# A two-layer decoder step: keys ahead of the last input units, queries scaled in PSUM reads, gates split inside attention, V pages by GpSimd, the norm unit by unit

## What is computed

```
for layer in (0, 1):
    h = rms_norm(x, g_mix)
    q, k, v, ... = split(h @ w_in)            # layer 0: forget gate, u, v_g; layer 1: gate_b, gate_c, h_in
    a = attention(q, cached pages + k, v)     # 0: softmax with forget sums; 1: stick-breaking
    b = u * spatial(layer_norm(v_g))          # 1: gate_b * short_conv(gate_c * h_in)
    x = x + concat(a, b) @ w_out
    x = x + square(relu(rms_norm(x, g_mlp) @ w_up)) @ w_down
y = rms_norm(x, g_final); k, v, forget gates and states are outputs as well
```

## Time and profile before

| | us |
|---|---|
| three runs, median (lowest, highest) | 1667.32 (1666.06, 1671.25) |
| the profiled execution, its span | 1666.99, 1665.3 |
| PE busy, of the span | 1542.4 (93%) |
| DVE, ACT, POOL busy | 729.8, 493.6, 57.9 |
| PE idle before matmuls, largest groups | 15.1 + 13.6 + 13.2 + 8.1 + 7.9 + 7.7 + 7.6 + 7.3 + 7.2 |
| mean granted clock | 0.965 |
| HBM read, written | 170.20 MB, 7.26 MB |

### The profile page before, as it was taken

One profiled execution on the slowest core, in us unless ns is written; L12 is line 12 of the kernel. 1 busy time (PEld: TensorE's weight loads), 2 busy tenths in 40 slices (PEclk: granted clock), 3 DMA queues, 4 the chain that ended last, 5 costly groups with the idle time before them and its releaser, 6 DMA issues.

```text
span 1665.3 us, 33771 instructions
## 1 busy us (share of the span) xinstructions
PE 1542.4 (93%) x13119; PEld 1445.1 (87%) x13119; DVE 729.8 (44%) x1267; ACT 493.6 (30%) x787; POOL 57.9 (3%) x130
## 2 busy tenths in 40 slices
PE   5879979978999999999999995987899999999997
PEld 5879946658999999999999994655799999999996
DVE  4335456534444333343443364656244433434333
ACT  4211234422333222231321113544233322313223
POOL 5420000000000000000000000000000000000000
PEclk9989989989999999999999998999899999999998
DMA  4323276762232222222222236677222332322222
GB/s 123 80 71 79 71 241 174 227 204 69 64 89 81 85 83 87 82 76 88 80 86 76 85 97 199 175 228 224 79 76 76 89 89 76 89 77 85 84 77 75
DMA packets 239740, 178.82 MB, mean 107 GB/s; under 512 B 9940, under 2 KB 203544, under 8 KB 239642
## 3 DMA queue, kind: packets, MB, share of 16 engines
q1 hardware_dynamic: 235546, 170.98, 35.3%
q0 software_dynamic: 4096, 6.52, 1.3%
HBM read 170.20 MB, written 7.26 MB: 107 GB/s over the span
## 4 chain that ended last, share of the span: by engine, by line
PE 81%; SPq 5%; issue 5%; DVE 2%; DMA 2%; POOLq 2%; POOL 1%; ACT 1%; DVEq 0%; ACTq 0%
PE B L1264 66%; PE B L1477 3%; PE B L1296 2%; SPq L372 2%; SPq L377 2%; PE B L1489 2%; PE B L1287 1%; POOLq L479 1%; PE B L1571 1%; PE B L1520 1%; PE B L1533 1%; PE B L1509 1%; POOL lf_raw L480 1%; SPq L390 1%; PE B L1364 1%
## 5 line engine op out<-in xcount | busy, mean ns | idle before, releaser
L541 ACT ACTIVATE WH<-WR 128x1024 fp32r<-128x1024 f32 x175 | 184.3, 1053 | 449.0 <-PE B L1264 448.9
L799 DVE TENSOR_TENSOR WL<-WR,WH 128x1024 fp32r<-128x1024 f32 x188 | 230.1, 1224 | 53.0 <-ACT WH L531 30.4
L1264 PE MATMUL B<-ffH,WH 128*128 128x288 f32 x1024 | 219.7, 295 | 0.0
L1264 PE MATMUL B<-ffL,WH 128*128 128x288 f32 x1024 | 218.0, 294 | 0.0
L1264 PE MATMUL B<-ffH,WL 128*128 128x288 f32 x1024 | 217.5, 293 | 0.0
L1264 PE MATMUL B<-H2H,WH 128*128 128x288 f32 x960 | 207.6, 297 | 6.2 <-issue 6.2
L1264 PE MATMUL B<-H2L,WH 128*128 128x288 f32 x960 | 206.0, 296 | 0.0
L1264 PE MATMUL B<-H2H,WL 128*128 128x288 f32 x960 | 205.3, 295 | 0.0
L1264 PE MATMUL B<-HH,WH 128*128 128x288 f32 x832 | 182.2, 301 | 16.8 <-issue 8.9
L1264 PE MATMUL B<-HL,WH 128*128 128x288 f32 x832 | 180.9, 300 | 0.0
L1264 PE MATMUL B<-HH,WL 128*128 128x288 f32 x832 | 180.6, 299 | 0.0
(11 more groups left out here) (292 smaller groups left out, 1659.2 us busy)
## 6 DMA issues: line engine op xcount, KB each, us to landing
WR<-in_w_up_dram SPq DMA_DIRECT2D x64, 512.0 KB, 4.0
WR<-in_w_down_dram SPq DMA_DIRECT2D x64, 512.0 KB, 3.8
WR<-in_w_in_odd_dram SPq DMA_DIRECT2D x24, 512.0 KB, 3.7
VR<-in_cache_fox_v_dram SPq DMA_DIRECT2D x44, 256.0 KB, 3.1
VR<-in_cache_sb_v_dram SPq DMA_DIRECT2D x44, 256.0 KB, 3.1
WR<-in_w_in_even_dram SPq DMA_DIRECT2D x20, 512.0 KB, 3.9
KR<-in_cache_fox_k_dram SPq DMA_DIRECT2D x32, 256.0 KB, 3.1
KRX<-in_cache_fox_k_dram SPq DMA_DIRECT2D x32, 256.0 KB, 3.0
```

What stands on the lines that cost most here:

```text
L541: A(WH[1 - u][:], WR[1 - u][:], ACT.Copy).then_inc(S["w_high"], 1)
L799: V.tensor_tensor(WL[u][:], WR[u][:], WH[u][:].bitcast(F32), ALU.subtract).then_inc(S["w_low"], 1)
L1264: last = M(B[2 * u + h][:, 0:TH], w[u][:, k, :], x[:, k, h * TH:(h + 1) * TH], start=(k == 0 and n == 0), stop=(k == KT - 1 and n == 2))
```

## The change

- **Norm.** `pair_across` runs the first unit in full, then the row sum, then the second. ACT and VectorE cut the third unit's weights before `norm` (in the first unit's body), in every stage. At the start unit 1 runs three chunks behind unit 0, only the first cut is waited for, and the constants are waited for ahead of the row sum.
- **Forget gates.** GpSimd issues 44 of the small loads, SP 20, between the weights of units 3 and 4 (`N_LFQ`).
- **Keys.** `turn_keys` runs before the last two q, k, v units, with a wait on PE for its copies; the K store follows at once.
- **Queries.** The first four q, k, v units are read from PSUM with the factor 1/8 and `R` in one operation; `QZ` has a place of its own and is filled after unit 7 (`fill_queries`).
- **Gates.** ACT and VectorE split two gate tiles at the end of slot 0 and two at the end of slot 1; the output projection waits for them.
- **Pages.** SP issues K pages alone, K 2 on after the K store has landed. GpSimd issues V pages: in layer 0 eight after the gates, in layer 1 eight during the side units; the rest after the V store. K has two buffers outside the shared space instead of four; the work buffers lie over `PB` 4 to 11 and `KN`.
- **Semaphore.** `evac_act` goes everywhere; VectorE's wait for the square is on `x_squared`.

The core of the diff (VectorE's halves of the norm change mirror ACT's; `load_v` moved from SP to GpSimd with its first four lines unchanged):

```diff
@@ -125,7 +125,8 @@
         v_feat_addr = arena + 2 * CT * T * 4
-        KR4 = place("KR", [P, 4, DA], F32)
+        KR2 = place("KR", [P, 2, DA], F32)
+        QZ = place("QZ", [P, CT, NB // 2, 2, 4 * NT], F32)
...
@@ -366,52 +368,38 @@
...
-                unit_loop(sp, load_weights(in_v[L], side + 2 * P), G_IN[L] + 2, n_b[L] - 2)
+                unit_loop(sp, load_weights(in_v[L], side + 2 * P), G_IN[L] + 2, 2)
+                if L == 0:
+                    for q in range(NPAGE - N_LFQ, NPAGE):
+                        v = sp.value_load(pages[0:1, q:q + 1], min_val=0, max_val=POOL - 1)
+                        sp.dma_start(lf_raw[q:q + 1, :, :], cache_fox_logf[0][ds(v, 1)]).then_inc(S["lfq_in"], 16)
...
                         sp.wait_ge(S[f"ring{L}"], RING_NO[L][("page", n - NK, 0)] + 1)
-                    elif n == 4:
-                        sp.wait_ge(S[f"q_block{L}"], 1)
+                    elif n == 2:
+                        sp.wait_ge(S["stored_kn"], 32 * (L + 1))
+                        if L == 0:
+                            sp.wait_ge(S["nat_turned0"], NG)
+                        else:
+                            sp.wait_ge(S["ue_set"], 1)
-                for n in range(NK):
+                for n in range(NPAGE):
...
-                for n in range(NV):
-                    load_v(L, n)
...
@@ -475,9 +463,25 @@
...
-            for q in range(NB * PG):
+            for q in range(NB * PG - N_LFQ):
...
+                if n >= NV:
+                    pool.wait_ge(S[f"v_used{L}"], n - NV + 1)
+                elif n == 8:
+                    if L == 0:
+                        pool.wait_ge(S["mixed"], CT)
+                        pool.wait_ge(S["stored"], 16 * 3)
+                    else:
+                        pool.wait_ge(S["conv_out"], CT)
+                    pool.wait_ge(S["stored_kn"], 32 * (L + 1))
...
@@ -500,6 +504,8 @@
                     pool.dma_start(prev_n[0:2 * NB, :], state_conv[0].rearrange("b r d -> (b r) d")).then_inc(S["state_in"], 16)
+                    for n in range(8):
+                        load_v(1, n)
@@ -508,10 +514,16 @@
                 pool.dma_start(tk_s[0].rearrange("b t h d -> (b t) (h d)"), KN[0:NS, TT, :]).then_inc(S["stored_kn"], 16)
+                if L == 0:
+                    pool.wait_ge(S["sgu_out"], CT)
+                    for n in range(8):
+                        load_v(0, n)
                 pool.dma_start(tv_s[0].rearrange("b t h d -> (b t) (h d)"), VN[0:NS, TT, :]).then_inc(S["stored_v"], 16)
+                for n in range(8, NPAGE):
+                    load_v(L, n)
...
@@ -562,7 +572,7 @@
                     split_high(z, i)
-                    A(TMP[:, u, :], X[:, i, :], ACT.Square).then_inc(S["evac_act"], 1)
+                    A(TMP[:, u, :], X[:, i, :], ACT.Square).then_inc(S["x_squared"], 1)
...
                     cut_high(k)
-            norm(0)
...
@@ -622,7 +625,14 @@
-                unit_loop(act, evac_in(pb_tile), G_IN[L], n_b[L], first_plain=True)
+                for u in range(2):
+                    evac_in(pb_tile)(G_IN[L] + u, u, u, "second" if u == 0 else None)
+                    if u == 0:
+                        norm(2 * L)
...
+                unit_loop(act, evac_in(pb_tile), G_IN[L] + 2, n_b[L] - 2, i0=2)
@@ -642,21 +652,23 @@
...
+                    unit_loop(act, evac_in(pa_tile), G_QKV[L] + 2, 8, i0=2)
...
-                    unit_loop(act, evac_in(pa_tile), G_QKV[L], 3 * CT)
-                name = "sgu" if L == 0 else "conv"
-                act.wait_ge(S["unit_done"], G_OUT[L] + 1)
-                for c in range(CT):
-                    act.wait_ge(S[f"{name}_out"], c + 1)
-                    A(HH[:, CT + c, :], PB[:, c, :], ACT.Copy).then_inc(S[f"{name}_high"], 1)
-                    if c == 1:
-                        copy_natural(NG if L == 0 else 0, len(NAT[L]))
+                    unit_loop(act, evac_in(pa_tile), G_QKV[L], 10)
+                k0 = NG if L == 0 else 0
+                copy_natural(k0, k0 + NG)
+                unit_loop(act, evac_in(pa_tile), G_QKV[L] + 10, 2)
+                copy_natural(k0 + NG, len(NAT[L]))
-                act.wait_ge(S[f"q_block{L}"], 2)
+                if L == 0:
+                    act.wait_ge(S["mixed"], CT)
+                    act.wait_ge(S["stored"], 16 * 3)
+                act.wait_ge(S["sgu_out" if L == 0 else "conv_out"], CT)
+                def gate_high(c):
+                    A(HH[:, CT + c, :], PB[:, c, :], ACT.Copy).then_inc(S["sgu_high" if L == 0 else "conv_high"], 1)
@@ -755,6 +767,9 @@
                     copy_ring("page", 4 * s + 3, 0)
+                    if s < 2:
+                        gate_high(2 * s)
+                        gate_high(2 * s + 1)
@@ -763,7 +778,6 @@
...
@@ -804,13 +825,18 @@
...
+            def evac_in(tile_of, b0=0, z=None, scale=None):
                     next_low(g, u, more)
+                    if z is not None and u == 0:
+                        norm(z)
...
+                        if scale is None:
...
+                        else:
+                            done = V.scalar_tensor_tensor(tile_of(i)[:, cols], B[b0 + 2 * u + h][:, 0:TH], scale, R[:, cols], ALU.mult, ALU.mult)
...
                             split_low(z, i)
-                        dve.wait_ge(S["evac_act"], g + 3)
+                        dve.wait_ge(S["x_squared"], z * KT + i + 1)
...
@@ -1041,38 +1068,41 @@
...
+                def fill_queries():
+                    if L == 0:
+                        V.memset(QZ[:], 0.0).then_inc(S["mask_set"], 1)
+                        dve.wait_ge(S["mask_set"], 6)
+                    else:
+                        V.memset(QZ[:], 0.0).then_inc(S["mask_set"], 1)
...
+                k0 = NG if L == 0 else 0
                 for i in range(3 * CT):
-                    evac_in(pa_tile)(G_QKV[L] + i, i, i % 2, "next")
+                    evac_in(pa_tile, scale=QS if i < CT else None)(G_QKV[L] + i, i, i % 2, "next")
                         steps[i]()
+                    if i == 7:
+                        fill_queries()
+                    if i == 9:
+                        copy_natural(k0, k0 + NG)
                     gate(3)
-                copy_natural(NG if L == 0 else 0, len(NAT[L]))
-                name = "sgu" if L == 0 else "conv"
-                for c in range(CT):
+                copy_natural(k0 + NG, len(NAT[L]))
+                cut_low(G_OUT[L] + 1, 1)
...
                     V.tensor_tensor(HL[:, CT + c, :], PB[:, c, :], HH[:, CT + c, :].bitcast(F32), ALU.subtract).then_inc(S[f"{name}_low"], 1)
-                cut_low(G_OUT[L] + 1, 1)
-                dve.wait_ge(S["stored_kn"], 32 * (L + 1))
...
-                V.memset(QZ[:], 0.0).then_inc(S[f"q_block{L}"], 1)
-                dve.wait_ge(S[f"q_block{L}"], 1)
-                dve.wait_ge(S[f"nat_act{L}"], nat_counts(L, "v")[1])
-                V.tensor_scalar(PA[:, 0:CT, 0:NP], PA[:, 0:CT, 0:NP], QS, None, ALU.mult)
...
@@ -1212,6 +1242,9 @@
                     copy_ring("page", 4 * s + 3, 0)
+                    if s < 2:
+                        gate_low(2 * s)
+                        gate_low(2 * s + 1)
...
                     pe.wait_ge(S["w_low"], g + 3)
-                    pe.wait_ge(S["evac_act"], g + (1 - behind))
...
                     pe.wait_ge(S["w_low"], g + 3 + u)
-                    for k in range(KT - 1):
+                    if u == 1:
+                        rms(z)
+                    for k in range(KT):
                         pe.wait_ge(S["h_low"], z * KT + k + 1)
-                        chunk(z, g, u, k, k == 0, False)
-                rms(z)
-                pe.wait_ge(S["h_low"], (z + 1) * KT)
-                for u in range(2):
-                    chunk(z, g, u, KT - 1, False, True)
+                        chunk(z, g, u, k, k == 0, k == KT - 1)
@@ -1336,16 +1368,23 @@
             turn_x(1)
-            pe.wait_ge(S["consts"], 1)
-            pe.wait_ge(S["w_low"], 4)
-            for k in range(KT):
+            LAG = 3
+            for k in range(KT + LAG):
                     turn_x(k + 2)
-                pe.wait_ge(S["h_low"], k + 1)
-                for u in range(2):
-                    chunk(0, 0, u, k, k == 0, k == KT - 1)
-            pe.wait_ge(S["x_copied"], 2 * KT)
-            rms(0)
+                if k < KT:
+                    pe.wait_ge(S["h_low"], k + 1)
+                    if k == 0:
+                        pe.wait_ge(S["w_low"], 3)
+                    chunk(0, 0, 0, k, k == 0, k == KT - 1)
+                if k == KT:
+                    pe.wait_ge(S["x_copied"], 2 * KT)
+                    pe.wait_ge(S["consts"], 1)
+                    rms(0)
+                if k >= LAG:
+                    if k == LAG:
+                        pe.wait_ge(S["w_low"], 4)
+                    chunk(0, 0, 1, k - LAG, k == LAG, k == KT + LAG - 1)
@@ -1364,11 +1403,19 @@
...
+                    k0 = NG if L == 0 else 0
```

(18 more changed lines are left out.)

123 lines of the change are left out of this document (56 added, 67 removed).

## The result

| | before | after |
|---|---|---|
| median (lowest, highest), us | 1666.89 (1666.06, 1671.25) | 1584.04 (1583.57, 1588.82) |
| the profiled execution's span, us | 1665.3 | 1581.9 |
| PE busy, us | 1542.4 | 1524.0 |
| span without PE, us | 122.9 | 57.9 |
| mean granted clock | 0.965 | 0.984 |

The ratio of the times is 0.9504, with a 95% interval from 0.948 to 0.9529: 82.9 us faster. 1583.5 was forecast. In the profiled executions the span is 83.4 us shorter: 65.0 us of PE's idle time went, and the same 13119 matmuls took 18.4 us less.

What follows compares the result with a forecast made beforehand. PE, busy 93% of the span, was taken as the bound, so only its waits and slow clock could be won. Terms summed to 83.8 us: 1667.0 - 83.8 + 0.3 = 1583.5 us; own bounds 1572 to about 1592, rivals' top 1608.

Steps and rivals of the forecast that it cites:

- the start: Kernel's start: unit 0 needs only the first cut, and the norm lies beside three chunks; 8.6 us, between 5.8 and 9.6.
- the norms: Later norms: the second unit covers the norm and the third unit's weight cut; three waits go, 9.3 us.
- the first pair: Output projection's first pair: PE waits only for the add into X, not ACT's square; two passes go, 2.8 us.
- the stages before attention: Turn into attention: keys turned before the last two units, query work moved earlier; 5.8 us and 5.1 us, sum 10.9.
- the pages: Inside attention: V pages by GpSimd and K pages ahead end the K waits, 13.2 + 13.6 = 26.8 us.
- forget gates: Before the log forget gates are turned: 20 of 64 small loads go to SP; the whole 7.2 us wait goes.
- the second block of a pair: Attention's second V block: its last four pages need 8.0 to 9.8 us of the 11.6 available, so it holds.
- the first rival: V pages late: last four land in 9.8 us, second V block waits 3.1 us eight times; 25 us, 1608; chance 0.18.
- The tail: Attention's very end: the last four V pages have nothing beside them; a loss of 1.3 us a layer, 2.6.
- The gates in the slots: Attention slots 0 and 1: gate splits queue ahead of page copies; new waits of 0.5 and 1.0 us, -1.5.
- Clock: Thirteen clock restarts behind waits that go; 22.3 us come back, from 0 to 22.3, taken whole.
- The rival that a third of VectorE's slack comes back as waits in layer 1: Layer 1's scans take back a third of 13.6, and half the clock's 22.3 stays: +15.6, 1599 us; chance 0.18.

Runs made afterwards that it cites:

- e_v_even: Changed kernel with V pages issued on SP again, from the ring's second turn in fours behind every fourth K page, not eights behind one: 1598.24 us, ratio 0.9574.
- e_gates_first: Changed kernel with the eight gate splits worked before attention again, none in slots 0 and 1: 1589.8 us, ratio 0.9516.
- e_pauses: Changed kernel with fourteen PE pauses, seven a layer, of 0 to 8 GpSimd clears (0.51 us each) between groups of eight MLP units: 1631.3 us, ratio 0.978.
- e_norm_back: Changed kernel with the second, third and fourth norm as before, the start staying changed: 1599.09 us, ratio 0.9577.

## Why the prediction was right

**What bounds the kernel.** PE's idle time and the slow clock behind it were all there was to win, as said: 65.0 and 18.4 us by the two traces. The terms for the start, the norms, the first pair and the stages before attention held in size and in mechanism; the largest, for the pages, held in size alone.

**Start, forget gates.** 8.6 against 8.4. PE starts at 14.81 (15.0 in the prediction) and turns the log forget gates at 77.86 ("about 77") without a wait. The miss is in "they are 22 us, over by about 41": SP's 20 loads took 24.2 us (20.00 to 44.23, 1.26 apart instead of 1.09), and the term left out what stands behind the last of them, unit 4's weights issued at about 44.6, some 4.7 us to land, and two passes to cut them. PE waited 1.2 us. It had no second price, being under 2 us, and went with the loads split in two tens.

**Norm, first pair.** 12.0 us against 12.1. Two passes of 0.69 are what went from each first pair: 3.98 became 2.59.

**Before attention.** 5.6 and 4.6 against 5.8 and 5.1. The new wait for the key copies is 0.73 in layer 0 and 0.95 in layer 1, where the sum has 0.65 for each. That "its few small passes lie under unit 8" held in layer 0 and not in layer 1: the fill stands there behind a convolution step and ahead of the next cut, and unit 9's weights were 1.00 late.

**Pages.** The term was right in size, 26.8, and its reason was wrong. "SP's queue is the bound in the waits" put them down to 128 issues of 1.09 us, 139.5 us a layer. e_v_even makes the same issues from the same queue and keeps 9.4 us of the waits, all of them behind the twelve V issues in a row near the start of the stage; the other 17.2 were the bursts of eight. It was the order in which one queue was written: tried for the 17.2, read from the rows for the 9.4. The edit took the waits away because it moved the V issues out of the K pages' way, and for that the size came out. I had the SP waits of the kernel before at hand and didn't use them. GpSimd's pitch, taken as 1.23, is 1.15 as in the small load, the lower bound:

```profile
251.96 0.54 POOL L483 DMA_DIRECT2D VRX<-in_cache_fox_v_dram  x1 [0.61 <-issue]
253.11 0.54 POOL L483 DMA_DIRECT2D VR<-in_cache_fox_v_dram  x1 [0.62 <-issue]
```

A page's issue takes 0.54 us, between the small load's 0.49 and the store's 0.79, and the pitch doesn't show it. The V pages land in 4.4 us (median), inside the 3.1 to 4.9 that I allowed, so the second block of a pair holds and the first rival fell.

**The mis-sized terms.** The tail was charged 2.6 us and cost 0.5: the V waits at the two ends are 2.6 us together and were 2.1. The prediction doesn't show where its 1.3 a layer comes from; four pages at a pitch longer by 0.06 are 0.2 us. The gates in the slots were charged 1.5 and cost nothing that shows: two new waits of 0.4 us for PP in layer 1 are there in e_gates_first too, which has no gates in its slots. A V wait of 1.5 us in the middle of layer 1 (at 1083.60), which was to stay, went. Against these stand those 0.8 us and 0.8 us of new waits for ACT's page copies at the start of layer 1, for which the sum has 0.4 ahead of attention. Together they are the 3.5 us by which attention did better.

**Clock.** 22.3 against 20.6 ("49 us, of which 46%" is 22.5). "I take it whole" was a little too much, and the place is layer 1's attention. By the prediction's shares the four restarts in each attention were worth about 7 us a layer. Layer 0 gave 7.0, layer 1 4.6: there PE still waits twice for 2.1 us, with a clock of 0.69 and 0.66 over the five us behind (0.66 and 1.00 behind the same waits before). The rival that a third of VectorE's slack comes back as waits in layer 1 fell: its attention idles 14.9 us, 13.3 less than before; layer 0 won 12.9. That most restarts gave their part back fits e_pauses: the waits that remain in the input stages behind the start are all under 1.6 us. (The wait at 862 us, behind which the clock stayed up, is the third of the four norm waits, not the second.)

## What to carry to other kernels

Before a queue is called a bottleneck, read what the queue itself waits for: a queue with K waits behind it and 19 us of its own waits needs another order first. And read where the waits stand that are left, not only whether their sum fits: here a sum for capacity matched, and the waits stood where capacity wasn't short. In a dense stream of matmuls like this one, price a wait of PE at its length up to about 1.5 us, and mostly at 1.5 to 2.7 us more when it is longer than two; so cutting a 3 us wait to 1 is worth more than it looks, and removing a 1 us wait less. Two units that share their last wait are better worked one after the other behind it than in turns, since the first one's end then hides the next weights' cut (2.6 us of wait became 0.2).

## What was not expected of the hardware

- An idle time of PE of 2.12 us was followed by the full clock once and by the lower one the other time, at the same place of the two layers. One of 3.1 us at layer 1's first norm was followed by 1.00 in the kernel before and by 0.50 in e_norm_back.
- 30 fp32 scalings by a constant back to back stopped a GpSimd DMA issue for 8.6 us, 60 of them for 18.9. 30 copies of the same size and 30 scalings by a column of SBUF made no issue longer than 0.77. Whoever issues DMAs from GpSimd should look for such trains on VectorE.
- GpSimd's pitch of DMA issues is 1.15 us for a 4 KB load and for a 256 KB page alike; only the instruction's own length differs (0.49 and 0.54).
